# Loading x already turned, folding the norm's gains and roots around the first projection, and loading finished position tables

## The reference

```python
hn = rms_norm(x, mix_pre_g)          # x * rsqrt(mean(x*x) + 1e-6) * g
proj = hn @ w_in                     # q 512 | k 128 | v 128 | u 1024
attn = sliding_window_attention(q, k, v, sinks, rel_bias)   # window 128, bias by distance
h = a * sigmoid(gate)                # a, gate = split(u)
h = depthwise_conv(h, 31 taps) + b   # causal
h = silu(layer_norm(h)) @ w_conv_pw
mixed = concat(attn, h) @ w_out
```

## Time and profile before

| | |
|---|---|
| median of 3 runs | 2306.9 us (2306.83 to 2306.95) |
| profiled execution: span | 2304.0 us, 2.9 us less than the median of the runs |
| PE / DVE / ACT / POOL busy | 2283.1 / 1402.2 / 974.5 / 867.9 us |
| chain that ended last | PE 94%, DVE 2%, ACT 2%, issue 1% |
| HBM read / written | 205.27 / 68.57 MB |

### The profile page before, as it was taken

The page is one execution under the profiler, slowest core; times in us unless marked ns, Lnnn a source line. Parts: engine busy times, 40 slices in busy tenths (PEclk is TensorE's granted clock), DMA queues, the critical chain, the costliest instruction groups (busy, mean ns, idle before and its releaser), DMA issues.

```text
span 2304.0 us, 30812 instructions
## 1 busy us (share of the span) xinstructions
PE 2283.1 (99%) x11636; PEld 1919.4 (83%) x11636; DVE 1402.2 (61%) x2229; ACT 974.5 (42%) x1988; POOL 867.9 (38%) x749
## 2 busy tenths in 40 slices
PE   8999999999999999999999999999999999999998
PEld 8788888888888888888898878888888888888887
DVE  7999715945444477776533676154594444447776
ACT  4126734433232344455634765135443323234543
POOL 2000235488787700033112032221448878770003
PEclk9999999999999999999999999999999999999999
DMA  5222134233233368665002001243223323336865
GB/s 160 53 64 79 51 102 145 65 119 119 87 120 105 126 243 285 209 220 136 20 10 71 24 10 37 67 171 111 101 68 108 124 86 127 103 119 247 291 214 194
DMA packets 219589, 275.85 MB, mean 120 GB/s; under 512 B 17259, under 2 KB 144972, under 8 KB 216626
## 3 DMA queue, kind: packets, MB, share of 16 engines
q1 hardware_dynamic: 200594, 210.31, 29.4%
q10 hardware_dynamic: 18848, 63.58, 7.0%
HBM read 205.27 MB, written 68.57 MB: 119 GB/s over the span
## 4 chain that ended last, share of the span: by engine, by line
PE 94%; DVE 2%; ACT 2%; issue 1%; DMA 0%; POOL 0%; SPq 0%; POOLq 0%; DVEq 0%; ACTq 0%
PE P L496 27%; PE P L498 27%; PE P L497 27%; PE P L3166 3%; PE P L3185 2%; PE P L3201 2%; PE P L508 1%; PE P L3123 1%; PE P L1523 1%; PE P L1549 1%; PE P L792 0%; ACT p L3264 0%; DVE stats L3334 0%; DVE s L1741 0%; PE P L1534 0%
## 5 line engine op out<-in xcount | busy, mean ns | idle before, releaser
L496 PE MATMUL P<-ah,wh 128*128 128x512 f32 (+1 forms) x1136 | 441.5, 389 | 1.1 <-POOL wl L462 0.5
L498 PE MATMUL P<-ah,wl 128*128 128x512 f32 (+1 forms) x1136 | 438.9, 386 | 0.0
L497 PE MATMUL P<-al,wh 128*128 128x512 f32 (+1 forms) x1136 | 438.7, 386 | 0.0
L496 PE MATMUL P<-wh,ah 128*128 128x512 f32 (+2 forms) x1128 | 426.0, 378 | 0.0
L498 PE MATMUL P<-wh,al 128*128 128x512 f32 (+2 forms) x1128 | 423.3, 375 | 0.0
L497 PE MATMUL P<-wl,ah 128*128 128x512 f32 (+2 forms) x1128 | 422.9, 375 | 0.0
L578 POOL TENSOR_TENSOR stats<-stats,epsc 128x1 f32<-128x1 f32 x78 | 31.5, 404 | 762.1 <-ACT xn L2012 420.9
L496 PEld LDWEIGHTS P<-ah,wh 128*128 128x128 f32 x1136 | 213.5, 188 | 44.9 <-ACT go L2510 0.8
L498 PEld LDWEIGHTS P<-ah,wl 128*128 128x128 f32 x1136 | 213.3, 188 | 43.4
L497 PEld LDWEIGHTS P<-al,wh 128*128 128x128 f32 x1136 | 213.5, 188 | 41.9
L498 PEld LDWEIGHTS P<-wh,al 128*128 128x128 f32 x1128 | 212.2, 188 | 37.0
(11 more groups left out here) (387 smaller groups left out, 4357.8 us busy)
## 6 DMA issues: line engine op xcount, KB each, us to landing
rf<-ff_rows SPq DMA_DIRECT2D x154, 256.0 KB, 5.3
stage<-in_w_down_dram SPq DMA_DIRECT2D x110, 256.0 KB, 3.9
ff_rows<-sb ACTq DMA_DIRECT2D x22, 1024.0 KB, 5.2
stage<-in_w_gu_dram SPq DMA_DIRECT2D x44, 512.0 KB, 5.0
stage<-in_w_in_dram SPq DMA_DIRECT2D x22, 512.0 KB, 4.0
stage<-in_w_gate_dram SPq DMA_DIRECT2D x22, 512.0 KB, 4.1
stage<-in_w_up_dram SPq DMA_DIRECT2D x22, 512.0 KB, 5.1
ff_rows<-uo ACTq DMA_DIRECT2D x22, 512.0 KB, 3.0
```

Of the source, the lines that this page charges most:

```text
L496: e.matmul(out, lh, rh, start=start, stop=False, skip_group_check=onto)
L497: e.matmul(out, lh, rl, start=False, stop=False, skip_group_check=onto)
L498: return e.matmul(out, ll, rh, start=False, stop=stop, skip_group_check=onto)
```

## The change

- Two layouts of x arrive: x as before, and x turned (`x_turned`, [128, 8, 1024]). The turned one is loaded in 256 KB and 512 KB pieces; ACT makes its high part with the gains as per-partition scale, DVE the low part. The eight normalizations, 64 transposes and their evictions go.
- The tokens' inverse roots are made by POOL for four tiles at once, turned by PE (four transposes for each token half), copied by DVE into `roots`, and multiplied into what the first projection gives: by DVE into each gate before the sigmoid, and by POOL into each sigmoid's result, and into k (four tiles), v and q0 to q3 after ACT's copy.
- The first weight chunk comes in two halves, DVE makes its low part, and the first group is one whole group of 512 columns.
- Bias tables are computed in layout on the host: `b1` and `b2` come by one load each and POOL negates them. The table products, their stores and the skewed loads go. The convolution's weights arrive turned.
- The numbers of taps between DVE's other duties change: 11 tap instructions fewer before the attention stage, which are then done at its steps 19 and 20.

```diff
-    lows_by_dve = {*range(1, 22), ...}
+    lows_by_dve = {*range(22), ...}
...
+    def x_turned_hi(k, th):
+        AC.e.activation(AH[:, k, cs], xt[:, k, cs], ACT.Copy, scale=gx[:, k:k + 1])
+    def x_turned_lo(k, th):
+        DV.e.scalar_tensor_tensor(AL[:, k, cs], xt[:, k, cs], gx[:, k:k + 1], AH[:, k, cs].bitcast(F32), ALU.mult,
+                                  ALU.subtract)
...
+    def token_roots_pe(th):
+        for t in range(4):
+            ins = PE.e.transpose(P[:, ROOT_BANKS[th], 128 * t:128 * t + 128],
+                                 col(80 + 4 * th + t).to_broadcast([128, 128]), ident[:, :])
...
     def mixer1_pe():
+        first_unit()
+        u_unit(0, 1, 0)
         u_unit(1, 0, 0)
+        token_roots_pe(0)
         u_unit(1, 1, 0)
+        for i in range(2):
+            u_unit(0, i, 1)
+        token_roots_pe(1)
+        for i in range(2):
+            u_unit(1, i, 1)
...
-                    for th in range(2):
-                        PE.wait_ge(cp, ("v", th))
+                    PE.wait_ge(tk, ("v", g))
...
     def mixer1_dve():
+        def gate(c, th):
+            e.tensor_tensor(SG[th][:, :], P[:, u_bank(c, 0, th), :], roots[:, 512 * th:512 * th + 512], ALU.mult)
         for c in range(2, 4):
             for th in range(2):
+                gate(c, th)
                 some_taps(6)
                 glu(c, th)
                 low_by_dve_to(2 * c + 3 + th)
-                some_taps(8)
+                some_taps(7)
...
     def mixer1_pool():
+        def gate(c, th):
+            PL.wait_ge(gl, ("u", c, th))
+            PL.e.tensor_tensor(SG[th][:, :], SG[th][:, :], roots[:, 512 * th:512 * th + 512], ALU.mult)
+        def scaled(name, th, tiles):
+            PL.wait_ge(cp, (name, th))
+            for tile in tiles:
+                ins = PL.e.tensor_tensor(tile, tile, roots[:, 512 * th:512 * th + 512], ALU.mult)
...
+        PL.wait_ge(l_b1, "all")
+        PL.e.tensor_scalar(b1[:, :, :], b1[:, :, :], -1.0, 1.0, ALU.mult, ALU.mult)
+        for name in KVQ:
+            for th in range(2):
+                if name == "k":
+                    scaled(name, th, [kp1[:, i, cs] for i in range(4)])
+                else:
+                    scaled(name, th, [v1t[:, cs] if name == "v" else q1[:, int(name[1]), cs]])
...
     def chunk_in_pool():
+        PL.wait_ge(l_b2, "all")
+        PL.e.tensor_scalar(b2[:, :, :], b2[:, :, :], -1.0, 1.0, ALU.mult, ALU.mult)
```

More of the change, by code:

```diff
@@ L98, in constants, with layouts @@
     ropek = np.concatenate([cos, cos, -sin, sin], 1).reshape(NT, 128, 64).transpose(1, 0, 2)
-    return {"c_ident": ident, "c_oh1": oh1, "c_oh2": oh2, "c_causal": causal,
+    return {"c_ident": ident, "c_causal": causal,
             "c_ropeq": np.ascontiguousarray(ropeq), "c_ropek": np.ascontiguousarray(ropek)}
+def layouts(given):
+    x = given["x"]
+    turned = x.T.reshape(8, 128, S).transpose(1, 0, 2)
+    gains = given["mix_pre_g"].reshape(8, 128).T
+    per_channel = np.concatenate([given["conv_dw"], given["conv_dw_b"][None], given["conv_ln_g"][None],
+                                  given["conv_ln_b"][None]], 0)
+    taps = per_channel.reshape(TAPS + 3, 4, 128).transpose(2, 1, 0)
+    p, j = np.arange(128)[:, None], np.arange(256)[None, :]
+    dist = 128 + p - j
+    row = np.where((dist >= 0) & (dist < 128), bucket_of(np.maximum(dist, 0)), 32)
+    near = np.concatenate([given["rel_bias"], np.full((1, 8), NEG, np.float32)], 0)[row].transpose(0, 2, 1)
+    j = np.arange(640)[None, :]
+    row = np.clip(512 + p - j, -63, 128) + 63
+    row = np.where(((p < 64) & (j >= 576)) | ((p >= 64) & (j < 64)), 192, row)
+    far = np.concatenate([given["rel_bias_2"][0], np.full((4, 1), NEG, np.float32)], 1)[:, row].transpose(1, 0, 2)
+    return {"x_turned": np.ascontiguousarray(turned), "x_gains": np.ascontiguousarray(gains),
+            "conv_taps": np.ascontiguousarray(taps), "near_bias": np.ascontiguousarray(near),
+            "far_bias": np.ascontiguousarray(far)}
 def block_kernel(nc, I, out):
@@ L301, in build @@
     l_t2 = [landing(f"l_t2{i}") for i in range(2)]
-    l_x0 = [landing(f"l_x0{i}") for i in range(6)]
-    l_sk = [landing(f"l_sk{i}") for i in range(3)]
+    l_x0 = [landing(f"l_x0{i}") for i in range(5)]
+    l_xt = [landing(f"l_xt{i}") for i in range(8)]
+    l_w0 = landing("l_w0")
     l_out = [landing(f"l_out{i}") for i in range(4)]
@@ L334, in build @@
     plan, first = weight_chunks(I, t2_dram)
-    lows_by_dve = {*range(1, 22), *range(first["chunk"], first["chunk"] + 4)}
+    lows_by_dve = {*range(22), *range(first["chunk"], first["chunk"] + 4)}
     chunk_done = {}
@@ L955, in rows_end_dve @@
         ps.norm_dve(NT - 2)
[L959 to L967, removed]
+    x0 = [big(f"x0_{i}", [128, 1024], kb) for i, kb in enumerate((68.5, 72.5, 76.5, 80.5, 32))]
+    xt = big("xt", [128, 8, 1024], 0)
     q1 = big("q1", [128, 4, 1024], 0)
@@ L988, in row @@
         def row(t):
[L989 to L998, removed]
+            if t >= 5:
+                SP.wait_ge(sq, ("x", t - 5))
@@ L999, in input_loads @@
+        e.dma_start(gx[:, :], I["x_gains"]).then_inc(*l_const.up("gx"))
+        for k in range(3):
+            turned_load(k, 1, 0)
+        first_piece(1, l_stage[0], 0)
+        loaded[0] = 1
+        for k in range(3, 8):
+            turned_load(k, 1, 0)
         load_to(1)
-        for t in range(3, 8):
+        for t in range(4):
             row(t)
+        e.dma_start(cwt[:, :, :], I["conv_taps"]).then_inc(*l_misc.up("taps"))
         load_to(2)
-        e.dma_start(cw[0:31, :], I["conv_dw"]).then_inc(*l_cw.up("taps"))
@@ L1018, in build @@
[L1018 to L1035, removed]
+        for t in range(4, 8):
+            row(t)
+        e.dma_start(sinks[:, :], I["attn_sinks"].partition_broadcast(128)).then_inc(*l_misc.up("all"))
     def mixer1_loads():
@@ L1041, in mixer1_loads @@
         after(SP, "u0")
-        for i in range(3):
-            SP.wait_ge(l_sk[i], "all")
-        skewed_load(b1, sk1, 8, 384, 256, l_b1)
+        e.dma_start(b1[:, :, :], I["near_bias"]).then_inc(*l_b1.up("all"))
         load_to(first["mem_k"] + 2)
     def x_square(t):
[L1048 to L1065, removed]
+        AC.wait_ge(l_x0[t % 5], t)
@@ new lines, in x_square, with x_root @@
+        AC.e.activation(x0[t % 5][:, :], x0[t % 5][:, :], ACT.Square, scale=RT, accum_out=col(64 + t)).then_inc(
+            *sq.up(("x", t)))
+    def x_root(th):
+        DV.wait_ge(sq, ("x", 4 * th + 3))
+        DV.e.tensor_scalar(col(72 + 4 * th, 4), col(64 + 4 * th, 4), EPS, None, ALU.add).then_inc(*sm.up(("x", th)))
+    def x_turned_hi(k, th):
+        cs = slice(512 * th, 512 * th + 512)
+        if th == 0 and k == 0:
+            AC.wait_ge(l_const, "gx")
+        AC.wait_ge(l_xt[k - k % 2 if th else k], (k - k % 2 if th else k, th))
+        AC.e.activation(AH[:, k, cs], xt[:, k, cs], ACT.Copy, scale=gx[:, k:k + 1]).then_inc(*ah.up(("x", k, th)))
@@ new lines, in x_turned_lo, with first_piece_hi @@
+    def x_turned_lo(k, th):
+        cs = slice(512 * th, 512 * th + 512)
+        if th == 0 and k == 0:
+            DV.wait_ge(l_const, "gx")
+        DV.wait_ge(ah, ("x", k, th))
+        DV.e.scalar_tensor_tensor(AL[:, k, cs], xt[:, k, cs], gx[:, k:k + 1], AH[:, k, cs].bitcast(F32), ALU.mult,
+                                  ALU.subtract).then_inc(*al.up(("x", k, th)))
+    def first_piece_hi(part):
+        AC.wait_ge(*((l_stage[0], 0) if part else (l_w0, "w0")))
+        AC.e.activation(WH[0][:, 512 * part:512 * part + 512], stage[0][:, 512 * part:512 * part + 512],
+                        ACT.Copy).then_inc(*wh.up(0 if part else "w0"))
@@ new lines, in first_piece_lo @@
+    def first_piece_lo(part):
+        ws = slice(512 * part, 512 * part + 512)
+        DV.wait_ge(wh, 0 if part else "w0")
+        DV.e.tensor_tensor(WL[0][:, ws], stage[0][:, ws], WH[0][:, ws].bitcast(F32), ALU.subtract).then_inc(
+            *wd.up(0 if part else "w0"))
+    ROOT_BANKS = (2, 3)
+    def token_roots_pe(th):
+        claim(ROOT_BANKS[th], ev, ("x_roots", th))
+        PE.wait_ge(l_cw, "ident")
+        PE.wait_ge(rs, ("x", th))
+        for t in range(4):
+            ins = PE.e.transpose(P[:, ROOT_BANKS[th], 128 * t:128 * t + 128],
+                                 col(80 + 4 * th + t).to_broadcast([128, 128]), ident[:, :])
+        ins.then_inc(*tp.up(("x_roots", th)))
@@ L1094, in turn_unit_matrix @@
[L1094 to L1108, removed]
-            e.matmul(P[0:4, TABLE_BANKS[i], 0:n], rb2b[:, :], oh2b[:, a:a + n], start=False, stop=True).then_inc(
-                *mm.up(("table", i)))
@@ L1112, in tables_dve, with first_unit @@
-    def tables_dve():
-        for i, (a, n) in enumerate(TABLES):
-            m = 8 if i == 0 else 4
-            DV.wait_ge(mm, ("table", i))
-            DV.e.tensor_scalar(tables[i][:, :], P[0:m, TABLE_BANKS[i], 0:n], -1.0, None, ALU.mult).then_inc(*ev.up(("table", i)))
+        freed = (ev, ("gate" if i == 0 else "u", c, th))
```

(75 more changed lines are left out.)

192 lines of the change are left out of this document (69 added, 123 removed).

## The result

The changed kernel takes 2332.0 us (median of 4 runs, 2331.8 to 2332.9), the kernel before 2306.9 in the same session (4 runs, 2305.9 to 2306.95): 1.0112 times as long, 95% interval 1.0099 to 1.0124. That is slower by 25.1 us; the prediction said 28.

The account below looks back on a forecast made before the run. PE and DVE end the projection together, and DVE, slowed by POOL, would set its end. 26.5 before the first scores plus 2.7 in attention, less about 1 for waits: 2306.9 + 28 = 2335 us, range 2312 to 2350.

Parts of the forecast that it names:

- first product with a gate: Projection, DVE: its first product with a gate, behind low parts, sigmoid and POOL's multiplication, at about 36.5 us, now 32.68.
- PE ends q3: Projection, PE: held by DVE's weight low parts and POOL's v, it ends the q3 group near 184 us.
- PE alone ends the projection: Projection: PE, if nothing else held it, would end at 167.1 us, 12 us sooner than now.
- DVE at the first scores without POOL: End of projection: DVE's own work, without contention from POOL, reaches the first scores at 174.0 us, 5.9 sooner than now.
- POOL's multiplications: Projection: 25 POOL instructions beside DVE's taps cost DVE 1.1 us each, 27.5 us, with 15 to 33 possible.
- b1's negation: Projection: POOL's negation of 2048 elements costs DVE 4.8 us, between 0 if hidden and 6.
- first scores: End of projection: DVE reaches the attention's first scores at 206.3 us, 26.5 later than now.
- attention stage: Steps 19 and 20: the 11 moved taps leave 2.7 us uncovered before the convolution's turn, between 0 and 4.
- later stages: After attention: POOL's negation of b2 costs 0, at most 2 us; dropped loads and stores gain 0 to 1.
- Taps aren't held: Rival, projection: POOL does not slow DVE's taps, so the change gains 3.2 us, 2303.7 us; chance 0.09.
- the gain in full: Rival, projection: PE's 12 us gain at the start arrives whole, taps not being awaited, 2295 us; chance 0.03.
- Taps shut POOL out: Rival, projection: DVE's taps keep POOL waiting, so v's turn and q groups come late, 2354 us; chance 0.09.

Follow-up runs that it names:

- narrowed taps, v first: Changed kernel with 108 later convolution instructions cut from 512 to 64 columns, and POOL scaling v before b1 and k; 2296.2 us.
- fills: Changed kernel with POOL's 26 multiplications by the roots replaced by constant fills of the 512-column tiles, scaling left out; 2307.55 us.
- negation on ACT: Changed kernel with b1 negated by ACT instead of POOL, nothing else changed; 2330.5 us.
- with v first: Changed kernel with POOL scaling v before it negates b1 and scales k, same work; 2332.1 us.
- with narrowed taps: 108 later convolution instructions cut from 512 to 64 columns: 2306.1 us on the kernel before, 2298.2 us on the changed kernel.
- the kernel that scales from PSUM: Changed kernel with DVE scaling k, v and q from PSUM and also multiplying the gates, and ACT negating b1; 2317.65 us.
- one-column kernel: Changed kernel with POOL's 26 multiplications by the roots cut to the first of 512 columns, b1's negation kept whole; 2307.7 us.

## Why the prediction was right

Step by step, as predicted and as measured (us):

| step | predicted | measured | from |
|---|---|---|---|
| first product | 6.9 | 7.89 | changed kernel |
| first product with a gate | 36.5 | 37.4 | changed kernel |
| PE ends q3 | 184 | 187.7 | changed kernel |
| PE alone ends the projection | 167.1 | 168.4 | narrowed taps, v first |
| DVE at the first scores without POOL | 174.0 | 175.1 | fills (176.86) less the negation's 1.8 |
| POOL's multiplications | +27.5 | +25.0 | changed kernel less fills |
| b1's negation | +4.8 | +1.8 | negation on ACT |
| first scores | 206.3 | 201.8 | changed kernel |
| attention stage | +2.7 | +4.2 | 26.16 - 21.97, changed less before |
| later stages | 0 | -0.2 | 26.0 - 26.16, changed less before |

- **What bounds.** That DVE would set the end, and PE's earlier start vanish into its waits, held in the kernels with fills, with v first and with narrowed taps.
- **The held taps.** The price of 1.1 from two starts 1.70 apart was nearly the right one: taps beside POOL start 1.67 to 1.71 apart, 0.66 alone, so 1.0 to 1.05 each. Their number was 23 and not 25, since three gates and not one fell into DVE's waits, which grew by 1.8. The mean of two lines of taps rose from 0.75 to 0.96 and 0.99, and of the third from 0.83 to 0.88, single ones to 1.75 to 1.79; the mean of 1 us, which the prediction had named as a sign, wasn't reached. The rule of the Trainium skill ("SBUF — State Buffer", section "Who interferes with whom"), that the holder keeps the port for the whole instruction, taken at its word made 32.5; the measured 25.0 is below it and below my 27.5 as well. Its other half, that only a reading GpSimd instruction contends, is what the fills show.
- **The negation was mis-sized.** I took POOL's time per element from low parts, whose lines are two-input; one of POOL's with a scalar takes less: 2.01 us for 2048 elements beside narrow taps, below. It cost DVE 1.8, nearly that whole length. b2's, predicted at 6.0 us for 2560 elements, took 2.33.
- **The attention stage was too low by 1.5.** The uncovered taps cost 2.2 (predicted 2.7). The rest, 2.0, goes with PE's clock, as far as the traces tell: with the waits its mean granted clock was 0.79 and 0.89 of the 2.4 GHz from 120 to 160 and from 160 to 200, and 0.50, the lower level, from 200 to 205. It stays there until 208:

```profile
204.00:208.00 4.00, 4.00 (x17) 3.53 (x17) 2.33 (x10) 2.52 (x13) 0.00 (x0) 0.51 0.98 366
208.00:212.00 4.00, 4.00 (x30) 3.70 (x28) 2.67 (x13) 3.22 (x11) 0.00 (x0) 1.00 0.75 244
```

  PE is full in both, with 17 instructions and with 30, which makes some 1.7 us by my estimate. In the kernel that scales from PSUM, PE doesn't wait for taps, and still the end is 1.7 later than the first scores' shift gives (14.8 against 13.1). I had put that at no more than 1. No run separates the clock from the rest of the stage: with narrowed taps and v first 1.4 us are lost there too, at a granted clock of 1.00 throughout. PE is busy for 9.9 of the 12 us from 180 to 192 in that kernel and for 11.4 in the kernel before with the same taps, and it waits more for ACT.
- **Luck.** The errors partly cancel: 3.0 (negation) and 2.5 (multiplications) too much; 1.1 (DVE without POOL) and 1.5 (attention) too little, and 1 that I subtracted for waits and that isn't found: 28 against 26.0 in the span. The last 0.9 to the 25.1 of the medians is the distance from span to median, 2.0 us and not the 2.9 that I had added.

**The rivals.** "Taps aren't held" and "the gain in full" fell with the taps' length. "Taps shut POOL out" fell as a price, but its mechanism is in the trace: b1's negation stands from 125.20 to 135.07 and the taps run unheld at 0.66 until 133.2. With v first it is v's scaling that stands for 15.14 us:

```profile
120.91 15.14 POOL L1416 TENSOR_TENSOR v1t<-v1t,token_roots 128x512 f32<-128x512 f32 x2 [7.30 <-ACT v1t L1298]
136.01 2.35 POOL L1439 TENSOR_SCALAR b<-b 128x2048 f32<-128x2048 f32 x1
```

It changed no time because PE had as long to wait for DVE anyway.

## What to carry to other kernels

Before work goes to an idle POOL, count the DVE instructions with two SBUF inputs that run beside it: here each POOL instruction with 512 columns read cost DVE 1.0 us, more than the 0.60 that DVE itself needs for the same product from PSUM. Two taps with one SBUF input were held as well. A gain at the start of a stage that two engines end together is worth nothing until the second one is relieved, and one that makes the second longer turns into a loss. The longest wait in a list need not be the cause: ask which engine has no gap.

## What the runs showed that was not expected

- **POOL enters late, then alternates.** When POOL issues into an unbroken run of taps it may stand for some 6 to 12 us (from 121.63 to 127.4 in the one-column kernel, from 120.91 to 133.1 with v first); once in, it gets a turn after every tap. With one column to do, two q instructions of POOL took 9.12 us:

```profile
143.27 9.12 POOL L1416 TENSOR_TENSOR q<-q,token_roots 128x1 f32<-128x1 f32 x2 [5.62 <-ACT q L1300]
...
150.45 1.22 DVE L475 TENSOR_TENSOR wl<-stage,wh 128x1024 fp32r<-128x1024 f32 x1
151.59 1.41 DVE L1201 SCALAR_TENSOR_TENSOR odd_taps<-hp,cwt,odd_taps 128x513 f32<-128x513 f32 x2
```

  The entry fell just behind DVE's low part of a weight chunk (ending at 133.2 in the changed kernel, at 133.1 with v first, at 151.6 here), but a pair that stood from 154.15 in this kernel was done at 160.96, before the next low part began (161.49), and other POOL instructions got in between two taps at once (88.75 to 90.48). What decides it is open; it was not tried.
- **POOL's price depends on its form.** Beside narrowed taps, an operation with a scalar took 0.98 ns per element and one with two tensors 12.61 / 8 / 512 = 3.1 ns:

```profile
120.10 2.01 POOL L1438 TENSOR_SCALAR b<-b 128x2048 f32<-128x2048 f32 x1 [12.52 <-DMA b<-in_near_bias_dram]
122.08 12.61 POOL L1417 TENSOR_TENSOR kp<-kp,token_roots 128x512 f32<-128x512 f32 x8
```
